# The nine places of a rotating weight store, kept to the end of two expert stages

## What is computed

```python
def expert(y, p):
    wg, wu, wd, ge = p           # (1024, 512), (1024, 512), (512, 1024), gates
    a = jax.nn.silu(t @ wg) * (t @ wu) * ge[:, None].astype(t.dtype)
    return y + a @ wd, None
y, _ = lax.scan(expert, jnp.zeros_like(t), (w_gate, w_up, w_down, gates.T))
```

## Time and profile before

| what | value |
|---|---|
| median of 3 runs | 1442.75 us (1440.75 to 1445.83) |
| the profiled execution, its own time | 1440.93 us |
| its span, first to last instruction | 1439.0 us |
| mean granted clock of TensorE | 0.983 |
| PE busy | 1354.5 us, 94% |
| DVE, ACT, POOL busy | 517.8, 282.2, 47.2 us |
| queue q1 (SP) | 319.19 MB, 60.4% of 16 engines |
| expert stage of layer 0, first to last product of experts | 348 to 600 us |
| expert stage of layer 1 | 1126 to 1412 us |

### The profile page before, as it was taken

The page is one execution under the profiler, slowest core; times in us unless marked ns, Lnnn a source line. Parts: engine busy times, 40 slices in busy tenths (PEclk is TensorE's granted clock), DMA queues, the critical chain, the costliest instruction groups (busy, mean ns, idle before and its releaser), DMA issues.

```text
span 1439.0 us, 17852 instructions
## 1 busy us (share of the span) xinstructions
PE 1354.5 (94%) x6816; PEld 768.3 (53%) x6816; DVE 517.8 (36%) x1376; ACT 282.2 (20%) x580; POOL 47.2 (3%) x63
## 2 busy tenths in 40 slices
PE   5899999997998999889999999999998998899997
PEld 2456556555444444447667567576565544444434
DVE  3145355625111111554464653744513311111123
ACT  3143344411010111231120221212111100001013
POOL 1001200000000000100000000100100000000010
PEclk9999999998999999999999999999999899999998
DMA  9967686926999999912323423224534799579891
GB/s 363 322 244 231 224 279 237 380 95 238 392 396 350 398 395 378 388 64 94 117 82 117 146 88 110 95 89 139 182 118 174 254 398 387 190 258 398 324 399 52
DMA packets 162742, 344.83 MB, mean 240 GB/s; under 512 B 5929, under 2 KB 23554, under 8 KB 162626
## 3 DMA queue, kind: packets, MB, share of 16 engines
q1 hardware_dynamic: 150320, 319.19, 60.4%
q10 hardware_dynamic: 9362, 14.37, 2.7%
q0 software_dynamic: 2944, 9.65, 2.5%
HBM read 324.96 MB, written 18.22 MB: 238 GB/s over the span
## 4 chain that ended last, share of the span: by engine, by line
PE 85%; DMA 6%; DVE 4%; ACT 2%; SPq 2%; issue 1%; DVEq 0%; ACTq 0%
PE psum L1089 14%; PE psum L771 11%; PE psum L786 10%; PE psum L808 9%; PE psum L1120 7%; PE psum L986 7%; PE psum L1206 5%; PE psum L937 3%; PE psum L1198 3%; DMA ring<-in_moe_w_up 3%; PE psum L673 2%; PE psum L1031 2%; DMA ring<-in_da_w_qkv 2%; SPq L569 1%; PE psum L1060 1%
## 5 line engine op out<-in xcount | busy, mean ns | idle before, releaser
L771 PE MATMUL psum<-hT,ring 128*128 128x384 f32 x512 | 173.5, 498 | 8.8 <-DMA ring<-in_da_w_qkv 5.9
L1089 PE MATMUL psum<-ring,work 128*64 128x512 f32 x384 | 170.1, 593 | 2.6 <-DMA ring<-in_moe_w_up 2.6
L1090 PE MATMUL psum<-ring,work 128*64 128x512 f32 x384 | 170.2, 594 | 0.0
L771 PEld LDWEIGHTS psum<-hT,ring 128*128 128x128 f32 x512 | 99.0, 195 | 77.4 <-issue 8.3
L808 PE MATMUL psum<-ring,hT 128*128 128x512 f32 x288 | 125.9, 593 | 0.0
L986 PE MATMUL psum<-work 128*128 128x128 f32 x768 | 106.4, 292 | 5.5 <-issue 3.5
L1089 PEld LDWEIGHTS psum<-ring,work 128*64 128x64 f32 x384 | 51.8, 137 | 111.2 <-issue 111.0
L986 PEld LDWEIGHTS psum<-work 128*128 128x128 f32 x768 | 95.0, 200 | 28.2 <-issue 24.0
L1120 PE MATMUL psum<-ring,work 128*64 128x512 f32 x192 | 89.9, 612 | 1.3 <-issue 1.2
L1975 DVE COPY work<-psum 128x512 f32<-128x512 f32 x32 | 22.1, 692 | 191.2 <-PE psum L1121 191.2
L1121 PE MATMUL psum<-ring,work 128*64 128x512 f32 x192 | 90.0, 613 | 0.0
(11 more groups left out here) (338 smaller groups left out, 1810.0 us busy)
## 6 DMA issues: line engine op xcount, KB each, us to landing
ring<-in_w_ada SPq DMA_DIRECT2D x24, 2048.0 KB, 12.4
ring<-in_moe_w_gate SPq DMA_DIRECT2D x24, 2048.0 KB, 13.0
ring<-in_moe_w_up SPq DMA_DIRECT2D x24, 2048.0 KB, 17.4
ring<-in_moe_w_down SPq DMA_DIRECT2D x24, 2048.0 KB, 17.9
ring<-in_da_w_qkv SPq DMA_DIRECT2D x6, 2048.0 KB, 14.8
sq<-in_moe_w_gate SPq DMA_DIRECT2D x8, 1536.0 KB, 12.3
hT<-in_moe_w_up SPq DMA_DIRECT2D x8, 1536.0 KB, 15.0
work<-in_moe_w_down SPq DMA_DIRECT2D x24, 512.0 KB, 11.3
```

The costliest lines, as they stand in the source:

```text
L771: last = mm(b[:, 0:TOK], w[:, kt, col:col + P], hT[:, kt, :], start=kt == 0, stop=kt == KT - 1)
L1089: mm(psum[0:BLK, x, :], xk, wg[kt], start=kt == 0, stop=kt == KT - 1)
L1090: last = mm(psum[BLK:P, x, :], xk, wu[kt], start=kt == 0, stop=kt == KT - 1)
```

## The change

`moe` keeps all nine places to the end. Units 0 to 38 go through the nine places in turn. The last nine follow a list, `tail`: units 39 to 41 (expert 13) go to the three spares, units 42 to 44 (expert 14) to the places that `order` has at 3 to 5, and units 45 to 47 (expert 15) to those at 0 to 2. No product, copy or byte is added or removed. The places of retention's units and of the second stage are renumbered so that they follow the order in which the slots come free.

```diff
-WHOLE = 3 * (NE - EPG)
...
-    order = ((2, 3, 0, 1, 4, 5), (4, 5, 2, 3, 0, 1))
+    order = ((2, 3, 0, 1, 4, 5), (4, 5, 1, 2, 3, 0))
     rest = []
 
     def turn_in():
 
-        units.extend(u + (order[0][i % RSLOT],) for i, u in enumerate(rest))
+        units.extend(u + ((1, 2, 3, 0)[i % RSLOT],) for i, u in enumerate(rest))
         rest.clear()
 
     def moe(l):
 
         wide = NSLOT + SPARES
+        tail = [6, 7, 8, 3, 4, 5, 0, 1, 2]
         for n in range(3 * NE):
-            place = n % wide if n < WHOLE else (n - WHOLE) % NSLOT
+            place = n % wide if n < 3 * NE - wide else tail[n - 3 * NE + wide]
             units.append((("moe", l, n), None, order[l][place] if place < NSLOT else place))
```

More of the change, by code:

```diff
@@ L227, in plan_units @@
     rest += [(("rwo", n), ("rwo", 2 * n + 1)) for n in range(4)]
-    assert len(rest) % RSLOT == 0 and WHOLE % (NSLOT + SPARES) == 0
+    assert len(rest) % RSLOT == 0
     turn_in()
```

## The result

The changed kernel takes 1457.16 us (median of 4 runs, 1455.62 to 1459.35), the kernel before 1442.96 us beside it: 14.2 us slower, a ratio of 1.0104, 95% interval 1.0084 to 1.0123. The direction was forecast, and the size was twice the forecast: 1450.0 us was predicted, with a range up to 1455. The profiled execution took 1455.62 us with a span of 1453.2 us, against 1440.93 and 1439.0 before.

The account below looks back on a forecast made before the run. PE, busy 94%, was taken to bound the kernel, with gains only from its weight waits. Terms 4.0 + 1.65 + 1.7 = 7.35 us on 1440.93 gave 1448.3, by the runs' median 1450.1; predicted 1450.0 us, range 1443 to 1455.

Parts of the forecast that it names:

- What bounds, and that the last group's loads are full: PE busy 94%; its only waits for expert weights are two for unit 46, 1.70 and 0.94 us; engines move 390 GB/s.
- The moved waits: Units 42 to 47 wait for less; 39 to 41 wait one expert longer, 39 issued at 533.45 and 1345.07, queue empty.
- The price of an empty queue: Hole in SP's loads ahead of unit 39: 4.4 us lost in stage 0, 7.9 us in stage 1.
- The balance: New holes less the closed old ones, ahead of unit 46: 2.6 us behind in stage 0, 1.3 in stage 1.
- What the deficit costs at unit 46: Remaining bytes share the engines with POOL's unmoved gathers, so unit 46 lands 4.0 us later in stage 0, 1.65 in stage 1.
- TensorE's clock: The longer wait at expert 15 brings one more fall of the clock in stage 0, 1.7 us; none counted in stage 1.
- The refilled hole: Rival: a hole costs 1.5 us less, so the change is 1 to 4 us slower, 1444 to 1447 us; chance 0.30.
- the vanished waits: Rival: if unit 38 is still under way at 39's issue, expert 15's waits go, 1436.7 to 1440.1 us; chance 0.05.
- That the change does nothing: Rival: unit 39's wait is met earlier than the slot table tells, nothing moves, 1442.75 us; chance 0.03.
- The rule of the Trainium skill on the first byte: About 0.6 us to first byte, so each hole 1.5 us shorter, sum about 1 us; worth 0.03 of 0.30.
- The upper case of the forecast: Upper ends of the holes, two clock falls: 10.8 us, 1453.6 us; forecast with this case 0.62.
- Covers: Expert 13 and (rv, 0) stay covered; expert 14's unit 43 may wait 0 to 0.5 us, no addition.

Follow-up runs that it names:

- e6: The kernel before with only units 39 to 41 waiting one expert later, for expert 11; units 42 to 47 wait as before: 1457.95 us, ratio 1.0101.
- e3: The changed kernel with one more wait on GpSimd: the gathers of expert rows start only once unit 46 has landed: 1445.9 us, ratio 1.0036.
- e4: The changed kernel with unit 42 loaded ahead of units 39 to 41 instead of behind them: 1440.03 us, ratio 0.9990.
- e2: The changed kernel with the new places in stage 1 alone; stage 0 waits as in the kernel before: 1451.67 us, ratio 1.0066.
- e1: The changed kernel with the new places in stage 0 alone; stage 1 waits as in the kernel before: 1447.96 us, ratio 1.0053.
- e5: The kernel before with one more wait on GpSimd: the gathers start only once unit 46 has landed: 1440.11 us, ratio 0.9984.
- e7: The changed kernel with unit 42 loaded ahead of units 39 to 41 and the gathers held until unit 46 has landed: 1439.63 us, ratio 0.9980.

## Why the prediction was wrong in size

- **What bounds, and that the last group's loads are full.** Right. Of the waits for expert weights only the two for unit 46 are there, before and after. That the change adds no instruction was wrong by a little: expert 13 in the spares takes five more DMAs a stage than in `ring`, and `e6`, without them, takes the same time.
- **The moved waits.** Right: 39 was issued one expert later with the queue empty (534.16 for 533.45 us), and `e6` shows that this is enough for all of the loss. In stage 1 it came 5.2 us after the forecast in the trace's own time, as everything came 7.1 us later there and the stall in front of expert 11 was 1.84 us shorter.
- **The price of an empty queue.** Right: beyond the time from the last landing to the next issue, the forecast took 3.95 and 3.9 us for a hole, and it was 3.8 - 0.1 = 3.7 in stage 0 (unit 38 landed at 513.18 + 20.9 = 534.1) and 6.2 - 2.0 = 4.2 in stage 1 (1328.06 + 20.2 = 1348.3). The holes themselves were smaller, 3.8 and 6.2 us for 4.4 and 7.9, as 39 was issued 0.1 and 2.0 us after that landing, for 0.45 and 4.0. The balance was 2.0 us behind and 0.4 ahead, for 2.6 and 1.3 behind.
- **What the deficit costs at unit 46. This is the step that failed**, at 4.0 and 1.65 us. Of these 2.6 and 1.3 us were the deficit itself and only 1.4 and 0.35 us the clash with the gathers. From the earlier trace rows and the rows of after, unit 46 landed 47.3 us after unit 38 in stage 0 before and 53.3 us after it (534.1, 587.4) in the changed kernel: 6.0 us later. In stage 1 it was 51.5 and 55.7 us: 4.2 us later. Up to unit 45 that is 2.3 us late and 0.7 us early, as above. The rest came between the landings of 45 and 46, which took 9.7 us for 6.0 and 10.5 us for 5.6. So the clash cost 3.7 and 4.9 us more than before, for 1.4 and 0.35. Three things in the term were off. It let only 0.7 and 0.2 MB move in the gathers' time. From the gathers' first packet (580.1 and 1395.3) to the landing of unit 46 SP's queue moved 1.38 and 1.49 MB, before 0.35 and 0.22. It took shares of 0.214 and 0.237 MB a us from the earlier trace rows, and they were 0.19 and 0.18. And it said that the gathers do not move. In time they hardly do, but against the queue they do. In stage 1 POOL issued the first one 46.3 us after unit 38's landing before, and 42.7 us after it in the changed kernel:

```profile
1387.37 0.98 POOL L2168 DMA_INDIRECT work<-expert_rows,work  x1 [359.59 <-DMA expert_rows<-work]
```

```profile
1391.01 0.98 POOL L2168 DMA_INDIRECT work<-expert_rows,work  x1 [356.39 <-DMA expert_rows<-work]
```

  The kernel before had its stall of 2.50 us and the slow clock behind it in that stretch, and the changed kernel had not. So PE and the gathers came 3.5 us earlier against the queue, and the clash hit unit 46 although the bytes were not behind any more. `e3`, with 4.3 and 5.0 us for the clash, carries most of the difference. In stage 0 PE's wait of 5.86 us meets the forecast of 5.7 by luck: unit 46 landed 7.1 us later in the trace's time, but PE came 3.0 us later too, with a granted clock of 0.72 over 575 to 580 us, where it was 1.00 before.
- **TensorE's clock.** Forecast one more fall, 1.7 us, in stage 0. There it fell, and the part of expert 15 from its first product to its transposes took 14.86 us for 13.22, 1.6 us more. But the fall behind those transposes, which stood in the earlier trace rows, did not come, and 1.5 us were won back. In stage 1, where none was forecast, that part took 16.06 us for 13.21, 2.85 us more, with a mean clock of 0.50 over 1400 to 1410 us, and the later fall stayed. Forecast 1.7, measured 0.2 and 2.9.
- **The sum.** Landing of unit 46 6.0 + 4.2 us for 4.0 + 1.65, clock 3.0 for 1.7, and 0.7 us of difference ahead of the first stage's end. Together 13.9 of the 14.2 us, for 7.35.
- **The rivals.** The refilled hole and the vanished waits did not come. That the change does nothing is excluded by the issue of unit 39. What the faster rival asked for, a unit still under way when 39 is issued, is nearly what `e4` supplied, and the waits did vanish, for 1.6 us of gain by the medians, inside the interval. The rule of the Trainium skill on the first byte ("DMA: Bandwidth & Descriptors", section "Latency and other measured facts") gave about 1 us for the change, by an estimate that took its 0.6 us to the first byte for the whole start. As a price of the hole the trace does not agree: it would be 2.4 us beyond the gap to the next issue, and was 3.7 and 4.2. For the first byte alone it does: the first packet of unit 39 ran at 535.20, 1.04 us after its issue began and 0.67 us after it ended (534.16 and 0.37). What the estimate leaves out is the time from there to the full rate. The upper case of the forecast, 1453.6, had the sizes of the holes and a second fall of the clock as its freedom, and missed the same step.
- **Covers.** Experts 13 and 14 and (rv, 0) show no wait in the changed kernel, as forecast.

Left open: the stall in front of expert 11 in stage 1. The traces show that it goes with the hole. In the four that have the hole in stage 1 (the changed kernel, `e2`, `e3`, `e6`) it is 0.66 to 1.10 us, in the five where the queue still moves weights at that time (before, `e1`, `e4`, `e5`, `e7`) 1.93 to 2.50 us. So it is less a matter of chance than of what the queue moves at the time. In all nine one packet of 16 KB of the instruction queue q8 ran 2.4 to 2.5 us before the stall's end, so it may be a load of TensorE's program; no run tests that. The fall of the clock behind it stands in two of the five only (before, `e4`). Open too is why SP's queue moved 17.8 and 17.5 MB between the landings of units 38 and 46 in the changed kernel, where the eight units have 16.8 MB and the kernel before moved 16.8 and 16.6: up to 1.0 MB of unit 47 went ahead of the end of 46. `e3` has this as well in stage 0 (17.6 MB), so the clash is not its reason.

## What to carry to other kernels

When the places of a rotating store are dealt out anew, do not count only how early each place comes free: walk the in-order queue and look at the first load whose wait gets longer, since a later release for one unit holds back all behind it, and one free unit moved ahead of it can fill the hole in whole or in part. A queue that runs a few us ahead of its reader has no reserve if other traffic starts at a fixed point of the work: here a deficit of 2 us came back as 6 us in stage 0, and in stage 1, with no deficit left, that traffic started 3.5 us earlier against the queue and the load came 4.2 us later. Price all bytes that are still to move up to the awaited load when that traffic starts, not the deficit alone, at the share that the queue has once both are active.

## What the runs showed of the hardware

While POOL's gathers ran, the queue of SP got a bit under half of the engines, 46 to 49% in the changed kernel and 53% before in 579 to 584 us, though it had two 2 MB loads waiting. A load that met the gathers took 4.3 to 5.0 us longer to land (26.87 and 28.26 us against 22.57 and 23.26). Around the end of a wait of PE of 8.65 us, which ended at 1404.11, the granted clock was 0.50 from 1400 to 1410 us, which is the lower level of 1.2 GHz, and the products ran at 1.1 us instead of 0.6 for some 6 us after PE was at work again.
